# A hybrid decoder block with 32 experts: raw rows to the router, one-pass rank products, selection first, and recurrence turns as transposes

## The reference

```python
p = rmsnorm(h, norm_mix_g) @ w_in                      # 1024 -> 3072 + 3360 + 2048
y_conv, y_rwkv = short_conv_mixer(...), rwkv7_time_mix(...)   # 16 heads of 64, a state of 64x64 each
h = h + (gate_conv * y_conv + gate_rwkv * y_rwkv) @ w_out
hn = rmsnorm(h, norm_ffn_g)
logits = hn @ router_w + router_b                      # 32 experts
top_val, top_idx = lax.top_k(logits, 4); gates = softmax(top_val)
# every token: sum over its 4 experts of gate * (clamped_swiglu(hn @ w1[e] + b1[e]) @ w2[e] + b2[e])
return rmsnorm(h + moe, norm_final_g)
```

## Time and profile before

| | us |
|---|---|
| median of 3 runs (1370.33 to 1371.29) | 1371.24 |
| the profiled execution, its own time | 1370.54 |
| its span, first to last instruction | 1368.7 |
| TensorE busy | 1267.5 |
| VectorE busy | 325.4 |
| ScalarE busy | 202.3 |
| GpSimd busy | 60.1 |
| mean granted TensorE clock | 0.976 |

### The profile page before, as it was taken

How to read it: one execution, slowest core, us unless ns; L and a number is a source line. 1 busy time by engine, 2 the same in 40 slices (tenths; PEclk the granted TensorE clock), 3 DMA queues, 4 the chain that set the end, 5 groups by cost and what they waited for, 6 DMA issues and landing times.

```text
span 1368.7 us, 23026 instructions
## 1 busy us (share of the span) xinstructions
PE 1267.5 (93%) x10309; PEld 683.9 (50%) x10310; DVE 325.4 (24%) x553; ACT 202.3 (15%) x319; POOL 60.1 (4%) x29
## 2 busy tenths in 40 slices
PE   6999999999997999998998999998999999989986
PEld 5887888899954343333333333333333333333332
DVE  1114384145533121121111121111111111111112
ACT  4113131121213110011000011000011000111001
POOL 0000000065201000000000000000000000000000
PEclk9999999999997999999999999999999999999998
DMA  8351353211184999999999999999999999999993
GB/s 305 125 183 62 124 185 123 80 52 27 31 364 174 414 433 426 430 436 432 430 429 427 430 434 431 431 428 430 433 432 429 429 430 429 435 431 433 430 425 132
DMA packets 41506, 449.79 MB, mean 329 GB/s; under 512 B 3984, under 2 KB 5008, under 8 KB 24976
## 3 DMA queue, kind: packets, MB, share of 16 engines
q1 hardware_dynamic: 39408, 445.58, 77.7%
q10 hardware_dynamic: 2048, 3.43, 0.9%
HBM read 447.95 MB, written 1.05 MB: 328 GB/s over the span
## 4 chain that ended last, share of the span: by engine, by line
PE 67%; DMA 30%; DVE 2%; ACT 1%; issue 1%; SPq 0%; DVEq 0%; ACTq 0%
DMA ring<-in_exp_w 29%; PE ps L653 20%; PE ps L393 17%; PE ps L686 10%; PE ps L447 4%; PE ps L619 3%; PE ps L610 3%; PE ps L555 2%; PE ps L456 2%; PE ps L449 2%; PE ps L664 1%; PE ps L643 1%; DVE work L1220 1%; PE ps L673 1%; PE ps L400 1%
## 5 line engine op out<-in xcount | busy, mean ns | idle before, releaser
L653 PE MATMUL ps<-ring,work 128*64 128x512 f32 x2048 | 469.4, 613 | 49.6 <-DMA ring<-in_exp_w 49.6
L653 PEld LDWEIGHTS ps<-ring,work 128*64 128x64 f32 x2048 | 151.3, 141 | 350.0 <-issue 273.9
L393 PE MATMUL ps<-work,ring 128*128 128x256 f32 (+1 forms) x1072 | 232.5, 379 | 0.6 <-ACT work L712 0.6
L686 PE MATMUL ps<-ring,work 128*64 128x512 f32 x1024 | 225.1, 592 | 0.0
L393 PEld LDWEIGHTS ps<-work,ring 128*128 128x128 f32 (+1 forms) x1072 | 202.1, 189 | 31.5 <-issue 2.0
L1209 DVE TENSOR_SCALAR work<-ps 128x512 f32<-128x512 f32 x32 | 22.1, 691 | 500.5 <-PE ps L653 500.5
L686 PEld LDWEIGHTS ps<-ring,work 128*64 128x64 f32 x1024 | 72.4, 136 | 129.7 <-issue 129.6
L864 ACT ACTIVATE work<-work 128x512 f32<-128x512 f32 x32 | 20.1, 629 | 739.2 <-DVE work L1209 739.2
L1225 DVE COPY work<-ps 128x512 f32<-128x512 f32 x32 | 22.1, 691 | 208.2 <-PE ps L686 208.2
L610 PEld LDWEIGHTS ps<-sel,work 128*128 128x128 bf16 x1584 | 56.3, 118 | 26.1 <-issue 24.3
L619 PE MATMUL ps<-work 64*128 64x512 f32 x264 | 65.6, 615 | 0.8 <-DVE work L1225 0.8
(11 more groups left out here) (218 smaller groups left out, 791.9 us busy)
## 6 DMA issues: line engine op xcount, KB each, us to landing
ring<-in_exp_w SPq DMA_DIRECT2D x64, 4096.0 KB, 29.2
ring<-in_exp_w SPq DMA_DIRECT2D x64, 2048.0 KB, 30.2
ring<-in_w_in SPq DMA_DIRECT2D x16, 2048.0 KB, 7.9
ring<-in_w_out SPq DMA_DIRECT2D x2, 2048.0 KB, 8.6
ring<-in_w_in SPq DMA_DIRECT2D x1, 1152.0 KB, 7.8
work<-in_x SPq DMA_DIRECT2D x2, 512.0 KB, 3.9
work<-in_x ACTq DMA_DIRECT2D x2, 512.0 KB, 5.2
out<-work SPq DMA_DIRECT2D x2, 512.0 KB, 2.6
```

The lines of the kernel that those rows point to most:

```text
L393: last = mm(ps[b % 4][0:width, 0:T], chunk(n)[:, k, c0:c0 + width], XN[:, k, :], start=k == 0, stop=k == KT - 1)
L653: last = mm(ps[4 + part][64 * half:64 * half + 64, :], xe[:, k * CAP:(k + 1) * CAP], ring[:, slot(u, k), part * D + half * 512:part * D + ...
L686: last = mm(ps[7][64 * half:64 * half + 64, :], lhs, ring[:, slot(u, 8 + j), i * D + half * 512:i * D + half * 512 + 512], start=False, st ...
```

## The change

Recurrence: each turn becomes 16 transposes; the upper and lower half of the partitions go to partitions 0 to 63 of two banks (`B` or `A`, and `X`), and ScalarE evicts them in two copies. Router: TensorE transposes the rows before the norm; the norm's weights are multiplied into the router's (`gcol`, on GpSimd), and the token's factor is applied to the logits. VectorE evicts one half of the transposed rows. Rank products are bf16, in one pass. On VectorE the masks come before ranks, the first expert's selection before rounds and gates. The first gather takes the second tile in fp32 from HN; its bf16 parts are made later. Zeroing is on GpSimd.

```diff
+        aboveb = flat(i_G2)[:, 1536:1600].bitcast(BF16)
+        onesb = flat(i_G2)[:, 1600:1664].bitcast(BF16)
+            def turn_apart(banks, src):
+                for m in range(KT):
+                    for q in range(2):
+                        last = nc.tensor.transpose(ps[banks[q]][0:HEAD, cols(m)], src(q, m), C("ident64", 64)[rows(q)])
+                return last
...
-                        pe.wait_ge(act_l[p], n_a + n - 6)
-                        turn(B[p], heads(src, c)).then_inc(pe_l[p], 1)
+                        pe.wait_ge(act_l[p], n_a + 2 * n - 13)
+                        turn_apart((B[p], X[p]), heads(src, c)).then_inc(pe_l[p], 1)
...
-                        turn(A[p], mat(mE[c])).then_inc(pe_l[p], 1)
                         if lv == 0:
-                            pe.wait_ge(act_l[p], n_a + 4)
+                            pe.wait_ge(act_l[p], n_a + 7)
+                        turn_apart((A[p], X[p]), mat(mE[c])).then_inc(pe_l[p], 1)
...
             out_product(1, 0, 0, 8).then_inc(wout_done, 1)
-            turn_hn(0)
+            turn_hb(0)
             out_product(1, 1, 0, 8).then_inc(wout_done, 1)
-            pe.wait_ge(late_in, 16 * 3)
-            route(0)
+            pe.wait_ge(rw_ready, 1)
+            route(0, 0)
             pe.wait_ge(wout_done, 2 * TT)
             pe.sem_inc(w_used, 4)
-            turn_hn(1)
-            route(1)
-            pe.wait_ge(dve_h, 6)
-            mm(ps[7][:, 0:E], C("above"), msk[:, 0, :], start=True, stop=True)
...
+            turn_hb(1)
+            route(0, 1).then_inc(pe_h, 1)
+            route(1, 0)
+            route(1, 1).then_inc(pe_h, 1)
...
+            pe.wait_ge(bf_consts, 2)
+            pe.wait_ge(dve_h, 5)
+            mm(ps[7][:, 0:E], aboveb, msk[:, 0, :], start=True, stop=True)
...
-            pe.wait_ge(h3_cast, 3 * TT)
-            gather()
+            pe.wait_ge(sel1f_ready, 1)
+            for k in range(KT):
+                o = ps[6][:, k * CAP:(k + 1) * CAP]
+                for s in range(3):
+                    mm(o, H3[:, 0, s, every_fourth(k)], sel[:, 0, :], start=s == 0, stop=False)
+                last = mm(o, HN[:, 1, every_fourth(k)], sel1f, start=False, stop=True)
+            last.then_inc(gathered, 1)
...
+                if u == 0:
+                    pe.wait_ge(h3_cast, 3 * TT)
...
+            act.dma_start(gcol[:], norm_ffn_g[0].rearrange("(k p) -> p k", p=P),
+                          allow_slow_non_contiguous=True).then_inc(late_in, 16)
...
-                        af(dst[:, :, toks(c)], by_m(ps[B[p]][:, :]), ACT.Copy).then_inc(act_l[p], 1)
+                        for q, bank in enumerate((B[p], X[p])):
+                            af(dst[rows(q), :, toks(c)], by_m(ps[bank][0:HEAD, :]), ACT.Copy).then_inc(act_l[p], 1)
...
+            root_of_squares(0, 8, 12, HN, dve_h, 1, act_h)
+            take_hb(0)
+            part(0, 0)
+            part(1, 0)
+            root_of_squares(1, 8, 12, HN, dve_h, 3, act_h)
+            take_hb(1)
+            part(2, 0)
+            part(0, 1)
+            act.wait_ge(dve_h, 6)
             af(ge[:, :, 0:TOP], ge[:, :, 0:TOP], ACT.Exp).then_inc(act_h, 1)
+            act.wait_ge(gathered, 1)
+            af(xe, ps[6][:, :], ACT.Copy).then_inc(xe_ready, 1)
+            part(1, 1)
+            part(2, 1)
...
+            ptt(rw, rw, gcol[:].unsqueeze(2).to_broadcast([P, KT, E]), ALU.mult).then_inc(rw_ready, 1)
+            left(0, 0)
+            left(0, 1)
+            pool.wait_ge(wout_done, 2 * TT)
+            nc.gpsimd.memset(yb, 0.0).then_inc(y_ready, 1)
+            nc.gpsimd.memset(gts, 0.0).then_inc(gt_ready, 1)
+            pool.wait_ge(sel1f_ready, 1)
+            left(1, 0)
+            left(1, 1)
...
-                v.wait_ge(act_h, 1 + 3 * t)
+                v.wait_ge(pe_h, 2 * t + 1)
+                cp(HNT[:, 0:4, t * P:(t + 1) * P],
+                   ps[(2, 6)[t]][:, :].rearrange("p (k n) -> p k n", k=4)).then_inc(hnt_half, 1)
+                v.wait_ge(act_h, 1 + 2 * t)
                 link(nc.vector.reciprocal(col[:, 14 + t:15 + t], col[:, 12 + t:13 + t]))
...
-                link(tt(lg[:, t, :], ps[4 + t][:, 0:E], rb, ALU.add))
+                link(stt(lg[:, t, :], ps[4 + t][:, 0:E], col[:, 14 + t:15 + t], rb, ALU.mult, ALU.add))
...
+            pick_rows(0)
+            ts(sel1f, C("slot", CAP), rk[:, 1, 0:1], None, ALU.is_equal).then_inc(sel1f_ready, 1)
+            pick_bias(0)
```

More of the change, by code:

```diff
@@ L489, in _ @@
                     pe.wait_ge(dve_l[p], n_d + 6)
-                    turn(B[p], heads(V, c)).then_inc(pe_l[p], 1)
+                    pe.wait_ge(blk_copied, len(blocks) + 24 - N_SHIFT)
+                    turn_apart((B[p], X[p]), heads(V, c)).then_inc(pe_l[p], 1)
                 for n, src in ((8, AA), (9, Kt)):
@@ L557, in out_product, with turn_hb, route @@
                 return last
-            def turn_hn(t):
-                pe.wait_ge(dve_h, 2 + 2 * t)
+            def turn_hb(t):
+                pe.wait_ge(dve_h, 1 + 2 * t)
                 for k in range(KT):
                     last = nc.tensor.transpose(ps[(2, 6)[t] + k // 4][:, (k % 4) * P:(k % 4) * P + P],
-                                               HN[:, t, k * P:(k + 1) * P], C("ident"))
+                                               HB[:, t, k * P:(k + 1) * P], C("ident"))
                     if k % 4 == 3:
                         last.then_inc(pe_h, 1)
-            def route(t):
-                pe.wait_ge(act_h, 3 + 3 * t)
-                for k in range(KT):
+            def route(t, half):
+                if half == 0:
+                    pe.wait_ge(hnt_half, t + 1)
+                else:
+                    pe.wait_ge(act_h, 2 + 2 * t)
+                for k in range(4 * half, 4 * half + 4):
                     last = mm(ps[4 + t][:, 0:E], HNT[:, k, t * P:(t + 1) * P], rw[:, k, :],
                               start=k == 0, stop=k == KT - 1)
-                last.then_inc(pe_h, 1)
+                return last
             pe.wait_ge(merged, 2)
@@ L771, in _ @@
                         act.wait_ge(pe_l[p], pair * NPE + 13 + 3 * lv)
-                        af(mPT[p], ps[A[p]][:, :], ACT.Copy).then_inc(act_l[p], 1)
+                        for q, bank in enumerate((A[p], X[p])):
+                            af(mPT[p][rows(q), :], ps[bank][0:HEAD, :], ACT.Copy).then_inc(act_l[p], 1)
                 if pair == 0:
@@ L1132, in _ @@
             v.wait_ge(late_in, 16 * 3)
+            v.wait_ge(gffn_in, 16)
+            v.wait_ge(b2_split, 6)
             for t in range(TT):
@@ L1149, in _ @@
+                link(tt(hot[:, t], C("expert", E).unsqueeze(2).to_broadcast([P, E, TOP]),
+                        mif[:, t, 0:TOP].unsqueeze(1).to_broadcast([P, E, TOP]), ALU.is_equal))
+                link(nc.vector.tensor_reduce(msk[:, t, :], hot[:, t], AX_X, ALU.max))
+            v.sem_inc(dve_h, 1)
+            v.sem_inc(u_free, 1)
             link(tt(ge[:, :, 0:TOP], mx[:, :, 0:TOP], mx[:, :, 0:1].to_broadcast([P, TT, TOP]), ALU.subtract))
             v.sem_inc(dve_h, 1)
-            for t in range(TT):
-                link(tt(hot[:, t], C("expert", E).unsqueeze(2).to_broadcast([P, E, TOP]),
-                        mif[:, t, 0:TOP].unsqueeze(1).to_broadcast([P, E, TOP]), ALU.is_equal))
@@ L1174, in _ @@
-            link(nc.vector.tensor_reduce(cnt[:, 4:5], ps[7][:, 2 * E:3 * E], AX_X, ALU.max))
-            link(ts(cnt[:, 5:6], cnt[:, 4:5], float(CAP), 1.0, ALU.is_gt, ALU.add))
-            for n in range(2, T // CAP):
-                link(stt(cnt[:, 5:6], cnt[:, 4:5], float(n * CAP), cnt[:, 5:6], ALU.is_gt, ALU.add))
-            link(cp(rounds[:], cnt[:, 5:6]))
-            v.sem_inc(rounds_in, 1)
-            n_rounds = v.value_load(rounds[0:1, 0:1], min_val=1, max_val=4)
-            v.sem_inc(u_free, 1)
@@ L1199, in _ @@
             pick_rows(0)
+            ts(sel1f, C("slot", CAP), rk[:, 1, 0:1], None, ALU.is_equal).then_inc(sel1f_ready, 1)
+            pick_bias(0)
+            link(nc.vector.tensor_reduce(cnt[:, 4:5], ps[7][:, 2 * E:3 * E], AX_X, ALU.max))
+            link(ts(cnt[:, 5:6], cnt[:, 4:5], float(CAP), 1.0, ALU.is_gt, ALU.add))
+            for n in range(2, T // CAP):
+                link(stt(cnt[:, 5:6], cnt[:, 4:5], float(n * CAP), cnt[:, 5:6], ALU.is_gt, ALU.add))
+            link(cp(rounds[:], cnt[:, 5:6]))
+            v.sem_inc(rounds_in, 1)
+            link(ts(rk[:, :, E:E + 1], rk[:, :, 0:1], -float(CAP), None, ALU.add))
+            v.wait_ge(act_h, 5)
+            link(nc.vector.tensor_reduce(cnt[:, 0:TT], ge[:, :, 0:TOP], AX_X, ALU.add))
+            link(nc.vector.reciprocal(cnt[:, 2:2 + TT], cnt[:, 0:TT]))
+            link(tt(ge[:, :, 0:TOP], ge[:, :, 0:TOP], cnt[:, 2:2 + TT].unsqueeze(2).to_broadcast([P, TT, TOP]), ALU.mult))
+            for t in range(TT):
+                link(tt(hot[:, t], hot[:, t], ge[:, t, 0:TOP].unsqueeze(1).to_broadcast([P, E, TOP]), ALU.mult))
```

(5 more changed lines are left out.)

97 lines of the change are left out of this document (42 added, 55 removed).

## The result

The changed kernel takes 1357.13 us (median of 4 runs, 1356.12 to 1358.79) against 1371.26 us for the kernel before beside it (4 runs, 1370.33 to 1375.46): a ratio of 0.9883 with a 95% interval of 0.9853 to 0.9912. Forecast were 1357.5 us and a range of 1349 to 1368. The profiled execution took 1356.47 us for a span of 1354.7 (1368.7 before): 14.0 us less. TensorE is busy for 1261.2 us, ScalarE for 215.5 (202.3 before; it now evicts each turn in two copies), VectorE for 325.4, GpSimd for 61.6.

A forecast was written before the change was run, and what follows sets the result against it. The experts' weight stream was taken as the bound, its end moving with its start or resumption. Turns 3.4 plus residual to first expert 10.3 made 13.7 us, from 1371.24 to 1357.5 us; range 1349 to 1368.

The forecast's parts named there:

- What bounds the kernel: Experts' weight stream at about 430 GB/s; the end moves one for one with the stream's start or resumption.
- The hole: Transfers idle about 20 us until the first expert's first four contraction blocks finish; still 9 us wide after the change.
- The turn: Recurrence's pair stages: 0.47 us of instructions plus 0.32 for two shape changes, 0.79 against 0.93; 24 turns save 3.4 us.
- rival a: Turns keep one array shape or hide the change: 0.47 us each, 11 us saved there, 1349.9 us; chance 0.18.
- rival (b): Row halves of a transpose don't run together: 1.25 us per turn, 7.6 us lost, 1368.5 us; chance 0.14.
- The copies: ScalarE evicts each turn in two copies, 24 x 0.60 us more, which stay hidden behind TensorE.
- rival c: Half clock enters the pair stages: alternating products and turns take 20.6 us more, 1378 us; chance 0.08.
- From the residual to the gather: Second tile's residual at 413.66, then masks at 419.9, ranks landed at 420.8, first gather at 421.6.
- The stall behind GpSimd: Before the masks, VectorE's 2.04 us subtraction ended with GpSimd's; it goes, as GpSimd's second-tile subtractions wait for the selection.
- The gather: First expert's gather, second tile in fp32: 3.1 us at full clock, 5.9 at half, 4.8 taken; ends at 426.4.
- Copy and first product as now: From gather's end to first expert 1.0 us, so it starts at 427.4 instead of 437.67: 10.3 us saved.
- Rival (d): Something holds the first expert all the same; only half of the 10.3 us come, 1362.5 us; chance 0.10.

The follow-up runs named there:

- Turns only: Kernel before with only the 24 turns of the pair stages made transposes, evicted in two copies each; 1366.41 us, ratio 0.9940.
- no turns: Changed kernel with the turns of the pair stages put back to products; 1365.77 us, ratio 0.9947.
- turns paired: Changed kernel with products of both chunks, then turns of both, for V, AA and Kt; 1359.80 us.
- GpSimd early: Changed kernel with GpSimd's second-tile subtractions no longer waiting for the first selection; 1358.46 us (one run).
- filler: Changed kernel with 13 more products of zeros on TensorE, ahead of the rank products and of the first gather; 1357.00 us.
- fp32 ranks: Changed kernel with the five rank products in fp32 again; 1367.87 us (one run).
- order and filler: Changed kernel with normed rows written in the gather's order, plus 13 more products of zeros on TensorE; 1355.11 us, ratio 0.9864.

## Why the prediction was right, by its steps

**What bounds the kernel: right.** The stream's rate is unchanged, R to end is 921.9 to 924.6 us in all kernels, and each shift of R is found in the end. "Turns only" and "no turns" show that the two places add (6.3 and 6.9 us by their medians, 14.1 together in the changed kernel). The hole stayed open: transfers are at 7 GB/s from 420 to 425, and resumed at 432.05 (forecast near 431).

**The turn: right in its make-up, mis-sized in one term.** 0.79 us was 0.47 for the instructions and 0.32 for two changes of shape; measured are 0.48 and 0.24. This makes 24 x (0.93 - 0.72) = 5.0 us instead of 3.4. The bound of 0.47 (rival a) was out, since the changes are real (turns paired); rival (b) was also out, since the halves overlap, and the cost without overlap is 0.97, not 1.25. Its 1.25 took 0.058 us for a transpose where the row it stood on gave 0.054, and both are above the 0.045 measured. The first load came 5.6 us earlier, though, not 5.0. P to Z lost 6.6 us: 6.1 between the first turn and the end of the levels (26.6 us in the first pair, 23.6 after), which is the 5.0, some 0.5 for the two turns of each pair that follow each other, and 0.6 without a name; and 0.5 ahead of the turns, where the pause of the second pair went (1.16 us) and the first pair's pauses grew (1.16 to 1.30 and 0.34). P came 0.2 later, and Z to L grew by 0.8, which is within what Z to L varies by.

**The copies: hidden, as forecast.** Until the turns are paired, when they are the next to be waited for.

**The clock in the pair stages (rival c): did not occur.** 1.00 from 280 to 350, though where turns and products alternate a third of the time (0.57 of 1.65 us) are transposes. The Trainium skill (TensorE: Matmul & The Clock Gate, Part 4) says that a transpose does not count as busy in the same way; by it the alternating stretches were at risk. No run here shows that: no profile has half clock where turns and products alternate.

**From the residual to the gather: right to 0.2 us.** Forecast were the masks at 419.9, the ranks at 420.8 and the gather at 421.6, all against a residual at 413.66: +6.2, +7.1, +7.9. Found: +6.4, +7.0 (VectorE adds the ranks at 415.05), +7.9. The stall behind GpSimd went with the order, as "GpSimd early" confirms by bringing it back, at 0.87 us.

**The gather: 5.26 instead of 4.8 us.** I had priced the strided fp32 load at 0.142 by the nearest row, L664, and twice that at half clock; it is 0.27 us, at either clock. I had also let the clock come back within the gather, and it did not. The forecast of 3.1 us at full and 5.9 at half clock is thus 4.8 and 5.3 (filler, after), and that 4.8 of mine came near is luck. The first expert comes 9.8 us earlier than before relative to the first load, against 10.3.

**The step that failed: the first expert.** "Copy and first product as now", and with it the conversion of an earlier expert into an earlier resumption one for one. I had kept the end of the half clock only as a bound of one cold microsecond. In the kernel before it ended with w1's beginning (437.2 against 437.67); now the expert starts while it lasts and w1's first half takes 9.8 us. That is 2.4 us. It also damps what is done ahead of it: of a shift of the expert inside the half clock, half reaches the resumption. (GpSimd early and fp32 ranks start it 0.9 us later and the resumption moved by 0.14 and by -0.07; that it was not 0.45 is the spread of the clock.) With the clock kept up (order and filler) those 2.4 us came back.

So 1357.5 was right by compensation, which is luck: turns 5.6 instead of 3.4, selection 7.4 instead of 10.3; stream and tail, forecast unchanged, gave 1.0 us more, which is within what R to end varies by. Rival (d), "something holds the first expert", was half right: nothing held it, but a slow first expert took a quarter of its gain.

## What to carry to other kernels

Where a transfer waits for an expert's progress and not for its start, price the work between start and release at the clock that the trace will grant there: work that is brought forward into a half clock stretch gives back half of the part that falls into it, and savings ahead of it are halved as long as it starts in there. A turn by transposes pays by the number of instructions and loses two changes of array shape; grouping them saves the change only if the engine that evicts them keeps up. When executions scatter by more than an edit is worth, compare lengths of stages between named events of both profiles, and look for kernels that are alike in a stage to know how good its length is: one repeat of the changed kernel agreed to 0.13 us in L to R, where five such kernels spread over 1.3.

## What the runs showed of the hardware

- An fp32 weight load of 128x128 whose columns are four elements apart takes 0.27 us (two in 0.54) at both levels of the clock. A block with contiguous loads takes 0.34 us against 0.58 at 2.4 GHz, and 0.64 against 0.66 at 1.2 GHz.
- VectorE's fp32 scalar_tensor_tensor over 128x1024 takes 1.28 us contiguous and 2.23 us (two halves) when it reads with a step of four.
- The first expert's w1 (64 fp32 products) takes 13.93 us at 2.4 GHz, and half of each microsecond at 1.2 GHz on top: 14.89 to 16.33 us in the nine profiles that had 1.9 to 4.8 us of it.
- While GpSimd ran a tensor_tensor of 2.12 us, a VectorE cast of 8 elements per partition took 0.92 us in place of 0.17, and five other operations of VectorE kept their length.
- Sixteen fp32 transposes of 64x64 take 0.48 us when the partition halves alternate, 0.25 us more when they don't; a change of array shape takes 0.12 to 0.13 us.
- The clock can fall while TensorE is busy without a gap. In the fp32-ranks execution, in the dense projections that no kernel here alters, the table by stage has:

```profile
124.00:132.00 8.00, 8.00 (x15) 3.49 (x14) 0.00 (x0) 1.15 (x3) 0.00 (x0) 0.50 0.00 0
```

against the kernel after in the same stretch:

```profile
124.00:132.00 8.00, 8.00 (x36) 6.55 (x36) 5.67 (x3) 1.15 (x3) 0.00 (x0) 1.00 0.00 0
```

TensorE is busy for all 8 us in both, with 15 instruction records against 36, and the clock is 0.50 against 1.00; the pair stages begin 10 us later (280.5 against 270.4). Ahead of the fall TensorE was busy without a gap from 90 us on, at 1.00. Three of the fourteen profiles have it, with P at 277.6, 280.3 and 280.5 us, and the other eleven P at 270.2 to 272.9. What sets it off no run here tells. In the fp32-ranks execution 8.6 us of the 10 are the clock's (0.82 from 120 to 122, 0.50 to 132, 0.60 to 140).
